# Two transformer blocks with a 32-expert layer: the experts' rows gathered already turned, in full precision, and six weight pieces loaded ahead instead of four

## The chip, the cores and the metric

The kernel runs on one core of a Trainium2 chip. The metric is the device time of one execution in microseconds (us); three runs are shown and the median counts. All times inside the execution are microseconds from the start of the profiled span.

## What is computed

The whole program is a first block of two mixers (gated spatial mixing with differential attention, then latent attention) over 512 tokens and 256 context rows, followed by a second block with grouped attention, retention and a mixture of experts. The change touches only the last stage, the experts:

```
grp_p = softmax(h @ w_grp + b_grp);  p_g, g_idx = top_k(grp_p, 1)
sel   = the 8 expert logits of that group
p_e, j_idx = top_k(softmax(sel), 2)                 # two experts a token
weights = p_g * (p_e / sum(p_e));  eid = g_idx * 8 + j_idx
...
y_blk = (silu(x_blk @ w_gate[e]) * (x_blk @ w_up[e])) @ w_down[e]
out[token] += y * weight
```

`h` is 512 tokens by 1024, all in f32; an expert has 512 hidden features, so its three matrices are 6 MiB in f32. There are 32 experts, and a token goes to two of them: 1024 assignments.

## The kernel before, in words

**Blocks.** Assignments are placed in blocks of 64 rows (`SLOT`). Blocks 0 to 31 belong to experts 0 to 31; what an expert gets beyond 64 rows goes to further blocks at the end. Blocks 0 to 29 are worked in 15 *pairs* (`PAIRS`), the rest as *singles*: block 30, 31 and, with the routing of these inputs, one more, 32 (33 first products in all).

**Weights.** An expert's matrices arrive as six pieces of 1 MiB (128 x 2048 f32), four for gate and up, two for down. The SP queue issues them. A ring of twelve buffers (`ring`, whose buffers have the tile names early, raw and ring) holds one pair. Four pieces are fetched before the experts start, the other eight once the earlier stages have freed their buffers. Then come `MORE` = 4 pieces of block 28, kept in four other buffers (`more`) until block 28 is worked, much later. After this, each ring buffer is filled again as soon as TensorE has used it (`s_used`, the loop at L688): SP waits for one piece, issues one transfer, and goes to the next. In the singles only the first six ring buffers are used (L701).

**Rows.** A block's rows are picked out of the normed rows `h2` (token tile m, 128 tokens on the partitions) by a one-hot matrix `hot` that VectorE makes (`one_hot`, L2047 and L2051). `in_product` contracts over the features, so it needs the rows turned, as `xe_t` (feature on the partition, row along it). Before the change this takes four steps for each pair (128 rows), or each single:

- once, ahead of the experts: ScalarE rounds `h2` to fp32r (`h2_high`, L1229), VectorE subtracts (`h2_low`, L1980), so that `h2h` + `h2l` are a high and a low part for fp32r products
- `gather(g, h)`, L2743: for each half h of the features, 4 token tiles x 2 parts = 8 products with `hot` stationary and 512 features moving, into one bank
- `gathered(g, h)`, L1248: ScalarE copies the bank to `xe_rows`
- `turn_rows(g, h)`, L2750: four transposes with the identity; `turned(g, h)`, L2078: VectorE copies to `xe_t`

**A pair on TensorE** (`pair(q, ...)`): `in_product` of block 2q (L2785, 16 f32 products, each two matmul records in the trace), `gather(q+1, 0)`, `turn_hidden` (L2794, two transposes of `hid`), `gather(q+1, 1)`, `out_product` (L2805, 8 products); then `in_product` of block 2q+1, `turn_rows(q+1, 0)`, `turn_hidden`, `turn_rows(q+1, 1)`, `out_product`. Between them ScalarE makes silu (L1252), VectorE multiplies (`hidden`, L2084), copies the turned `hid_t` (`hidden_turned`, L2088) and scales the output (`out_rows`, L2093). The result is stored to `pair_dram` by ScalarE's queue, for singles by GpSimd's. In `out_product` TensorE waits for `s_ht`, that is for the copy of L2088.

**The end.** After the last pair a table `late` is turned, the singles follow, the store of single 31 is awaited, GpSimd gathers all tokens' rows back from `pair_dram` (L872), and the last single's rows are added by a product (L2865). Then come the final norm and the stores.

Of the kernel before, what the change touches and what calls it, by code (L numbers as in the profile page):

```python
# [10 lines left out]
ALU = mybir.AluOpType  # L11
# [38 lines left out]
MORE = 4  # L50
# [253 lines left out]
def build(nc, src, out):  # L304
# [8 lines left out]
    with ExitStack() as stack:  # L313
# [67 lines left out]
        for g in range(2):  # L381
# [37 lines left out]
        h2h = at("h2h", xt_base, 0, [P, LT, D], F32R)  # L419
        h2l = at("h2l", xt_base, 16 * KB, [P, LT, D], F32R)  # L420
        h2_t = at("h2_t", xt_base, 32 * KB, [P, KT, SEQ])
        xe_rows = at("xe_rows", g_base, 16 * KB, [P, D])
        xe_t = at("xe_t", g_base, 44 * KB, [P, KT, P])
        hot = at("hot", xt_base, 40 * KB, [P, LT, P], F32R)
# [39 lines left out]
            ((gate_base, 0), (xt_base, 32), (g_base, 0), (g_base, 8)))]  # L464
# [100 lines left out]
        s_mods, s_row2, s_h2h, s_h2l = sem("s_mods"), sem("s_row2"), sem("s_h2h"), sem("s_h2l")  # L565
# [10 lines left out]
        s_first_hot, s_hot, s_gat, s_rows, s_turned, s_xt = (sem(n) for n in (  # L576
            "s_first_hot", "s_hot", "s_gat", "s_rows", "s_turned", "s_xt"))
# [72 lines left out]
        def _(sp):  # L650
# [230 lines left out]
        def _(act):  # L881
# [345 lines left out]
            def h2_high(m):  # L1227
                act.wait_ge(s_row2, m + 1)
                own.free(nc.scalar.activation(h2h[:, m, :], h2[:, m, :], ACT.Copy), s_h2h)  # L1229
# [15 lines left out]

            def gathered(g, h):
                act.wait_ge(s_gat, 2 * g + h + 1)
                nc.scalar.activation(xe_rows[:, 512 * h:512 * h + 512], ps[:, h, :], ACT.Copy).then_inc(s_rows, 1)  # L1248
# [15 lines left out]
            gathered(0, 0)  # L1264
            gathered(0, 1)
            act.wait_ge(s_blocks, 1)
            over = act.value_load(blocks_i[0:1, 40:41], min_val=0, max_val=BLOCKS - EXPERTS)
            with act.Fori(0, PAIRS) as q:
                silu(2 * q, 0)
                gathered(q + 1, 0)  # L1270
                gathered(q + 1, 1)
                store(2 * q, 0)
                silu(2 * q + 1, 1)
                store(2 * q + 1, 1)

            def single(o, nxt):
                silu(o + SINGLE, 0)
                if nxt:
                    gathered(o + PAIRS + 1, 0)
                    gathered(o + PAIRS + 1, 1)  # L1280
# [16 lines left out]
        def _(dve):  # L1297
# [679 lines left out]
            def h2_low(m):  # L1977

                dve.wait_ge(s_h2h, m + 1)
                own.free(nc.vector.tensor_tensor(h2l[:, m, :], h2[:, m, :], h2h[:, m, :].bitcast(F32), ALU.subtract), s_h2l)  # L1980

            for m in range(LT - 1):
                h2_low(m)

# [34 lines left out]
            h2_low(LT - 1)  # L2019
# [25 lines left out]
            def one_hot(g):  # L2045
# [4 lines left out]
                for m in range(LT):  # L2050
                    ins = nc.vector.scalar_tensor_tensor(hot[:, m, :], col, rel[:, bass.ds(8 * g + 4 + m, 1)],  # L2051
                                                         hot[:, m, :].bitcast(F32), ALU.is_equal, ALU.add)
# [23 lines left out]
            def turned(g, h):  # L2076
                dve.wait_ge(s_turned, 2 * g + h + 1)
                nc.vector.tensor_copy(xe_t[:, 4 * h:4 * h + 4, :], ps[:, 2 + h, :].rearrange("p (k n) -> p k n", k=4))\  # L2078
                    .then_inc(s_xt, 1)
# [50 lines left out]
            def single(o, nxt):  # L2130
# [46 lines left out]
        def _(pe):  # L2177
# [633 lines left out]
            pe.wait_ge(s_h2h, LT)  # L2811
            pe.wait_ge(s_h2l, LT)
            gather(0, 0)
            gather(0, 1)
            turn_rows(0, 0)
            turn_rows(0, 1)
# [3 lines left out]
            def pair(q, landed):  # L2820
# [18 lines left out]
            def single(o, nxt):  # L2839
                landed = single_piece(o)  # L2840
                in_product(o + PAIRS, 0, landed)
                if nxt:
                    gather(o + PAIRS + 1, 0)
                turn_hidden(o + SINGLE, 0)
                if nxt:
                    gather(o + PAIRS + 1, 1)
                out_product(o + SINGLE, 0, landed)
                if nxt:
# [133 lines left out]
```

## Time and profile before

| | |
|---|---|
| median of 3 runs | 1719.63 us (1715.76 to 1721.85) |
| span of the profiled execution | 1721.2 us, which lies within the runs |
| TensorE busy | 1585.1 us, 92% |
| VectorE / ScalarE / GpSimd busy | 927.7 / 517.6 / 157.0 us |
| expert stage, first in_product to the end | 1201.7 to 1721.2 us |
| transfers | 353.09 MB, 422 to 423 GB/s from 1240 to 1640 us |

The results give no time for the profiled execution apart from its span. Engines are TensorE (PE), its weight load (PEld), VectorE (DVE), ScalarE (ACT), GpSimd (POOL) and SyncE (SP). Matmul records overlap in the trace, so spacing between starts tells more than the duration of a record. A full-precision f32 product is two records of the same line.

### The profile page before, as it was taken

The numbers are of one execution on the slowest core, as the hardware profiler recorded it, in microseconds if no ns is written. First come the engines' busy times: TensorE is split into PE (matmuls) and PEld (weight loads), VectorE is DVE, ScalarE is ACT, GpSimd is POOL, SyncE is SP. The second block draws the span as 40 slices with busy tenths as digits, with TensorE's granted clock in tenths as the row PEclk, the third lists the DMA queues.
The fourth block names the chain that finished last, engine by engine and source line by source line (L and its number), as shares of the span: only waits on it lengthen the run. The fifth ranks groups of instructions, "written<-read, shape, count | busy, mean of one in ns | idle before, by whom it ended". The sixth has DMA issues, their size and how long they took to land.

```text
span 1721.2 us, 22873 instructions
## 1 busy us (share of the span) xinstructions
PE 1585.1 (92%) x8534; PEld 1112.6 (65%) x8534; DVE 927.7 (54%) x1602; ACT 517.6 (30%) x823; POOL 157.0 (9%) x203
## 2 busy tenths in 40 slices
PE   6699999979899999999999989899999898898995
PEld 6588887768688877878778868776434233333331
DVE  3877445466557854657679789777222212112124
ACT  3322221266615234454352368323000000000011
POOL 2000010013401100000132040110000000000003
PEclk9899999959999999999999999999999999999999
DMA  9132244300321421041445201257999999999995
GB/s 382 55 147 98 98 154 180 126 30 13 135 98 51 164 92 50 1 159 55 164 168 196 98 1 50 99 230 318 388 423 423 423 422 422 422 423 422 423 383 216
DMA packets 57620, 353.09 MB, mean 205 GB/s; under 512 B 7376, under 2 KB 7632, under 8 KB 20544
## 3 DMA queue, kind: packets, MB, share of 16 engines
q1 hardware_dynamic: 43200, 307.41, 44.6%
q0 software_dynamic: 9248, 35.63, 5.6%
q10 hardware_dynamic: 5088, 8.92, 1.4%
q8 instruction: 55, 0.90, 0.2%
q14 instruction: 29, 0.24, 0.0%
HBM read 332.53 MB, written 23.59 MB: 207 GB/s over the span
## 4 chain that ended last, share of the span: by engine, by line
PE 59%; DMA 16%; DVE 12%; ACT 5%; issue 3%; SPq 3%; POOL 1%; ACTq 0%; DVEq 0%; POOLq 0%
DMA early<-in_experts 11%; PE ps L2241 10%; PE ps L2243 10%; PE ps L2242 10%; PE ps L2785 7%; PE ps L2295 4%; PE ps L2805 3%; PE ps L2448 3%; PE ps L2743 2%; SPq L688 2%; PE ps L2472 2%; PE ps L2207 2%; PE ps L2465 1%; DMA early<-in_ada 1%; ACT p L966 1%
## 5 line engine op out<-in xcount | busy, mean ns | idle before, releaser
L2241 PE MATMUL ps<-whi,xth 128*128 128x512 f32 (+1 forms) x768 | 301.0, 392 | 3.1 <-DVE xtl L1712 1.8
L2243 PE MATMUL ps<-whi,xtl 128*128 128x512 f32 (+1 forms) x768 | 297.7, 388 | 0.0
L2242 PE MATMUL ps<-wlo,xth 128*128 128x512 f32 (+1 forms) x768 | 297.6, 387 | 0.0
L2785 PE MATMUL ps<-early,xe_t 128*64 128x512 f32 x904 | 207.6, 598 | 31.7 <-DMA early<-in_experts 25.9
L2785 PEld LDWEIGHTS ps<-early,xe_t 128*64 128x64 f32 x904 | 60.8, 136 | 172.6 <-issue 104.4
L2241 PEld LDWEIGHTS ps<-whi,xth 128*128 128x128 f32 x768 | 145.7, 190 | 33.6 <-DVE xtl L1712 3.5
L2243 PEld LDWEIGHTS ps<-whi,xtl 128*128 128x128 f32 x768 | 145.5, 190 | 29.5
L2242 PEld LDWEIGHTS ps<-wlo,xth 128*128 128x128 f32 x768 | 145.9, 190 | 28.3
L2084 DVE TENSOR_TENSOR hid<-hid,ps 128x256 f32<-128x256 f32 x33 | 13.9, 421 | 252.2 <-ACT hid L1252 252.2
L1308 DVE TENSOR_TENSOR wlo<-raw,whi 128x2048 fp32r<-128x2048 f32 (+3 forms) x52 | 103.2, 1984 | 71.4 <-ACT whi L893 70.7
L1252 ACT ACTIVATE hid<-ps 128x256 f32<-128x256 f32 x33 | 12.7, 385 | 392.5 <-PE ps L2785 392.5
L893 ACT ACTIVATE whi<-raw 128x2048 fp32r<-128x2048 f32 (+2 forms) x46 | 85.5, 1859 | 121.9 <-DMA raw<-in_even 34.1
L1355 DVE SCALAR_TENSOR_TENSOR raw<-raw,cvec 128x512 f32<-128x512 f32 x140 | 105.2, 752 | 5.0 <-DMA raw<-in_ada 0.2
L1601 DVE TENSOR_REDUCE stat<-ps 128x1 f32<-128x768 f32 x64 | 61.2, 957 | 55.8 <-PE ps L2465 51.4
L2093 DVE TENSOR_TENSOR tmp<-ps,gt 128x512 f32<-128x512 f32 x33 | 22.8, 692 | 105.7 <-PE ps L2805 105.7
L2805 PE MATMUL ps<-raw,hid_t 128*64 128x512 f32 x288 | 65.8, 598 | 0.6 <-DVE hid_t L2088 0.6
L723 POOL TENSOR_SCALAR stat<-stat 128x1 f32<-128x1 f32 (+3 forms) x39 | 18.5, 474 | 492.7 <-ACT xtl_f L1001 132.5
L2743 PE MATMUL ps<-h2h,hot 128*128 128x512 f32 x144 | 60.2, 418 | 0.0
L2743 PE MATMUL ps<-h2l,hot 128*128 128x512 f32 x144 | 56.5, 393 | 0.0
L1355 DVE SCALAR_TENSOR_TENSOR acc<-raw,cvec,acc 128x512 f32<-128x512 f32 x70 | 52.6, 752 | 2.9 <-DMA raw<-in_ada 0.4
L863 POOL DMA_DIRECT2D pair_dram<-tmp x4 | 2.2, 562 | 507.8 <-DVE tmp L2093 507.8
L1057 ACT ACTIVATE po<-ps,stat 128x768 f32<-128x768 f32 x32 | 28.9, 902 | 64.1 <-DVE stat L1601 64.1
(464 smaller groups left out, 2786.9 us busy)
## 6 DMA issues: line engine op xcount, KB each, us to landing
early<-in_experts SPq DMA_DIRECT2D x128, 1024.0 KB, 26.4
raw<-in_experts SPq DMA_DIRECT2D x51, 1024.0 KB, 25.2
raw<-in_ada SPq DMA_DIRECT2D x40, 1024.0 KB, 6.5
ring<-in_experts SPq DMA_DIRECT2D x15, 1024.0 KB, 27.7
raw<-in_even SPq DMA_DIRECT2D x14, 1024.0 KB, 5.1
raw<-in_second SPq DMA_DIRECT2D x10, 1024.0 KB, 5.2
early<-in_ada SPq DMA_DIRECT2D x8, 1024.0 KB, 18.2
pair_dram<-tmp ACTq DMA_DIRECT2D x60, 128.0 KB, 6.9
```

The source lines that it names most:

```text
L893: own(nc.scalar.activation(whi[:, k % SPLIT, 0:w], raw[:, number[splits[k]["name"]] % RAW, 0:w], ACT.Copy), s_hi)
L1308: own(nc.vector.tensor_tensor(wlo[:, k % SPLIT, at_], raw[:, g % RAW, at_], whi[:, k % SPLIT, at_].bitcast(F32), ALU.subtract), s_lo if pa ...
L1355: ins = nc.vector.scalar_tensor_tensor(dst, w[kt // 4][:, kt % 4, :], cv, dst, ALU.mult, ALU.add)
L1601: own(nc.vector.tensor_reduce(st[:, 1:2], v[:, 0:TOK], AX, ALU.max, negate=True), nb)
L2241: nc.tensor.matmul(v, a[0], b[0], start=first, stop=False)
L2242: nc.tensor.matmul(v, a[0], b[1], start=False, stop=False)
L2243: return nc.tensor.matmul(v, a[1], b[0], start=False, stop=last)
L2295: mm = nc.tensor.transpose(v[:, to:to + P], rows_, ident[:])
L2448: mm = nc.tensor.matmul(v[:, TOK:TOK + n], pts[w % 2][:, P * a:P * a + P], v_of(w, a), start=a == 0, stop=a == NT - 1)
L2743: mm = nc.tensor.matmul(ps[:, h, :], hot[:, m, :], part[:, m, 512 * h:512 * h + 512], start=m == 0 and part is h2h, stop=m == LT - 1 and p ...
L2785: mm = nc.tensor.matmul(ps[SLOT * t:SLOT * t + SLOT, 4 + s, :], xe_t[:, 2 * i + k, SLOT * s:SLOT * s + SLOT], w[:, D * k + 512 * t:D * k + ...
L2805: mm = nc.tensor.matmul(ps[SLOT * t:SLOT * t + SLOT, 7, :], hid_t[:, s, P * c + SLOT * k:P * c + SLOT * k + SLOT], w[:, D * k + 512 * t:D ...
```

## The change

`h2h`, `h2l` and `xe_rows` are gone, with the ScalarE and VectorE steps that made them. `gather` now has `h2` stationary (128 tokens x 128 features) and `hot` moving (128 or, in the singles, 64 columns), both in f32, and writes the turned rows straight into the bank from which `turned` copies: 2 halves x 4 feature groups x 4 token tiles = 32 products for each group of rows. In a pair the first half is gathered after the first block's `in_product`, the second after the second block's. `in_product` waits for each half of `xe_t` apart. In the singles `turned` copies 64 columns of each feature group. `MORE` is 6, the first four of these buffers lie where `h2h` and `h2l` were, and are waited for differently.

```diff
-MORE = 4
+MORE = 6
...
         more = [at(f"more{i}", base, offset * KB, [P, PIECE]) for i, (base, offset) in enumerate(
-            ((gate_base, 0), (xt_base, 32), (g_base, 0), (g_base, 8)))]
+            ((xt_base, 0), (xt_base, 8), (xt_base, 16), (xt_base, 24), (gate_base, 0), (xt_base, 32)))]
...
+            def kept(i):
+                sp.dma_start(more[i][:], src["experts"][SINGLE - 2, i]).then_inc(s_more, 16)
+
+            for i in range(3):
+                kept(i)
+            sp.wait_ge(s_sqn, SQUARED["h2", NT - 1])
+            kept(3)
             sp.wait_ge(s_row2, LT)
-            sp.dma_start(more[0][:], src["experts"][SINGLE - 2, 0]).then_inc(s_more, 16)
+            kept(4)
             filled(sp, "router")
-            sp.dma_start(more[1][:], src["experts"][SINGLE - 2, 1]).then_inc(s_more, 16)
-            for i in (2, 3):
-                sp.wait_ge(s_h2l, 2 * i - 2)
-                sp.dma_start(more[i][:], src["experts"][SINGLE - 2, i]).then_inc(s_more, 16)
+            kept(5)
...
-            turned_h2(2)
-            turned_h2(3)
-            h2_high(0)
-            h2_high(1)
-            turned_h2(4)
-            h2_high(2)
-            turned_h2(5)
-            h2_high(3)
+            for m in range(CT, NT):
+                turned_h2(m)
...
-                    turned(o + PAIRS + 1, 0)
-                    turned(o + PAIRS + 1, 1)
+                    turned(o + PAIRS + 1, 0, SLOT)
+                    turned(o + PAIRS + 1, 1, SLOT)
...
-            def gather(g, h):
-                pe.wait_ge(s_hot, g + 1)
-                for m in range(LT):
-                    for part in (h2h, h2l):
-                        mm = nc.tensor.matmul(ps[:, h, :], hot[:, m, :], part[:, m, 512 * h:512 * h + 512],
-                                              start=m == 0 and part is h2h, stop=m == LT - 1 and part is h2l)
-                mm.then_inc(s_gat, 1)
-
-            def turn_rows(g, h):
-                pe.wait_ge(s_rows, 2 * g + h + 1)
+            def gather(g, h, n=P):
+                if h == 0:
+                    pe.wait_ge(s_hot, g + 1)
                 for k in range(4):
-                    mm = nc.tensor.transpose(ps[:, 2 + h, P * k:P * k + P],
-                                             xe_rows[:, 512 * h + P * k:512 * h + P * k + P], ident[:])
+                    for m in range(LT):
+                        mm = nc.tensor.matmul(ps[:, 2 + h, P * k:P * k + n],
+                                              h2[:, m, 512 * h + P * k:512 * h + P * k + P], hot[:, m, 0:n],
+                                              start=m == 0, stop=m == LT - 1)
                 mm.then_inc(s_turned, 1)
...
-                pe.wait_ge(s_xt, 2 * g + 2)
                 for i in range(4):
+                    if i % 2 == 0:
+                        pe.wait_ge(s_xt, 2 * g + (i // 2 + 1))
...
             def pair(q, landed):
                 in_product(q, 0, landed)
                 gather(q + 1, 0)
                 turn_hidden(2 * q, 0)
-                gather(q + 1, 1)
                 out_product(2 * q, 0, landed)
                 in_product(q, 1, landed)
-                turn_rows(q + 1, 0)
+                gather(q + 1, 1)
                 turn_hidden(2 * q + 1, 1)
-                turn_rows(q + 1, 1)
                 out_product(2 * q + 1, 1, landed)
```

TensorE, last pair, from the end of the second block's `in_product` to its `out_product`. Before:

```order
L2785 MATMUL ps<-early,xe_t 64x512 [waits s_ew9]
L2785 MATMUL ps<-early,xe_t 64x512 x3
L2750 MATMUL ps<-ident,xe_rows 128x128 [waits s_rows]
L2750 MATMUL ps<-ident,xe_rows 128x128 x3
L2794 MATMUL ps<-ident,hid 128x128 [waits s_hid]
L2794 MATMUL ps<-ident,hid 128x128
L2750 MATMUL ps<-ident,xe_rows 128x128 [waits s_rows]
L2750 MATMUL ps<-ident,xe_rows 128x128 x3
L2805 MATMUL ps<-early,hid_t 64x512 [waits s_ew10,s_yev,s_ht]
```

The same place with the change (L2752 is in_product, L2715 gather, L2761 turn_hidden, L2772 out_product):

```order
L2752 MATMUL ps<-early,xe_t 64x512 [waits s_ew9]
L2752 MATMUL ps<-early,xe_t 64x512 x3
L2715 MATMUL ps<-hot,h_119 128x128 x16
L2761 MATMUL ps<-ident,hid 128x128 [waits s_hid]
L2761 MATMUL ps<-ident,hid 128x128
L2772 MATMUL ps<-early,hid_t 64x512 [waits s_ew10,s_yev,s_ht]
```

Eight transposes on both sides of `turn_hidden` became sixteen products ahead of it, and nothing stands between `turn_hidden` and the product that waits for `s_ht`. The first block of a pair now has the same order.

SP, from the last ring pieces to the loop. Before:

```order
L677 DMA ring_143<-in_experts 128x2048
L679 DMA more_144<-in_experts 128x2048 [waits s_row2]
L681 DMA more_145<-in_experts 128x2048 [waits s_mm2]
L684 DMA more_146<-in_experts 128x2048 [waits s_h2l]
L684 DMA more_147<-in_experts 128x2048 [waits s_h2l]
L688 ISA [waits s_used]
```

With the change:

```order
L673 DMA ring_140<-in_experts 128x2048
L676 DMA more_141<-in_experts 128x2048
L676 DMA more_142<-in_experts 128x2048
L676 DMA more_143<-in_experts 128x2048
L676 DMA more_144<-in_experts 128x2048 [waits s_sqn]
L676 DMA more_145<-in_experts 128x2048 [waits s_row2]
L676 DMA more_146<-in_experts 128x2048 [waits s_mm2]
L689 ISA [waits s_used]
```

Two more transfers stand ahead of the loop that fills the ring again, and three of them wait for nothing.

TensorE in the loop of singles, after the last products of `out_product`. Before:

```order
L2805 MATMUL ps<-raw,hid_t 64x512 x3
L2748 ISA
L2750 MATMUL ps<-ident,xe_rows 128x128 [waits s_rows]
L2750 MATMUL ps<-ident,xe_rows 128x128 x3
L2748 REGISTER_ALU
L2750 MATMUL ps<-ident,xe_rows 128x128 [waits s_rows]
L2750 MATMUL ps<-ident,xe_rows 128x128 x3
L2852 ISA
```

With the change, from the end of `turn_hidden`:

```order
L2761 MATMUL ps<-ident,hid 128x128
L2715 MATMUL ps<-hot,h_119 128x64 x16
L2772 MATMUL ps<-raw,hid_t 64x512 [waits s_ew4,s_yev,s_ht]
L2772 MATMUL ps<-raw,hid_t 64x512 x3
L2772 MATMUL ps<-raw,hid_t 64x512 [waits s_ew5]
L2772 MATMUL ps<-raw,hid_t 64x512 x3
L2810 ISA
```

The transposes after a single's `out_product` are gone; the second half's sixteen products, of 64 columns, stand ahead of it.

## Rows read from the trace of the kernel before

**Rows 1.** The page, share of busy transfer engines in 40 slices of 43 us.

```profile
DMA  9132244300321421041445201257999999999995
```

**Rows 2.** Windows: length; busy time (count) of PE, PEld, DVE, ACT, POOL; clock; DMA; GB/s.

```profile
1340.00:1600.00 260.00, 230.59 (x1034) 87.86 (x1034) 50.61 (x130) 16.72 (x34) 0.00 (x0) 1.00 1.01 423
```

**Rows 3.** Timeline of TensorE: first piece of pairs 5 and 6, idle time and its releaser.

```profile
1337.67 1.94 PE L2785 MATMUL ps<-early,xe_t 128*64 128x512 f32 x8 [0.35 <-DMA early<-in_experts]
...
1368.69 1.94 PE L2785 MATMUL ps<-early,xe_t 128*64 128x512 f32 x8 [0.46 <-DMA early<-in_experts]
```

**Rows 4.** Chain that ended last, start and length: first gather, pairs 0, 1, 14.

```profile
1195.84 3.69 PE ps L2743 x16
1201.73 7.09 PE ps L2785 x32
...
1229.01 6.87 PE ps L2785 x32
1235.88 2.04 PE ps L2743 x8
1238.14 1.85 PE ps L2743 x8
1239.99 3.58 PE ps L2805 x16
1243.58 6.89 PE ps L2785 x32
1252.44 3.65 PE ps L2805 x16
1256.09 6.87 PE ps L2785 x32
...
1616.42 6.87 PE ps L2785 x32
```

**Rows 5.** Timeline, last single: turn_hidden, its copy, out_product, nothing between them.

```profile
1688.72 0.44 PE L2794 MATMUL ps<-ident,hid 128*128 128x128 f32 x2 [1.04 <-DVE hid L2084]
1689.20 0.42 DVE L2088 COPY hid_t<-ps 128x256 f32<-128x256 f32 x1 [0.53 <-PE ps L2794]
1689.75 3.65 PE L2805 MATMUL ps<-raw,hid_t 128*64 128x512 f32 x16 [0.59 <-DVE hid_t L2088]
```

**Rows 6.** Timeline of TensorE and its weight loads: f32 products with 128 weights' columns.

```profile
1101.67 0.46 PE L2650 MATMUL ps<-state,qw_t 128*128 128x128 f32 x2 [0.72 <-issue]
...
1108.67 0.39 PE L2651 MATMUL ps<-vr,sw 128*128 128x128 f32 x2
...
1101.86 0.30 PEld L2651 LDWEIGHTS ps<-vr,sw 128*128 128x128 f32 x2
...
660.36 2.94 PE L2448 MATMUL ps<-v_o,pto 128*128 128x128 f32 x24
```

**Rows 7.** Chain: the router's products (36 columns moving). Timeline: products with 64 weights' columns.

```profile
1175.82 3.51 PE ps L2700 x32
...
1082.16 1.53 PE L2584 MATMUL ps<-ptg,kk 128*64 128x128 f32 x24 [0.26 <-ACT tmp L1185]
```

**Rows 8.** Windows of 2 us around the first refill of the ring.

```profile
1200.00:1202.00 2.00, 0.93 (x6) 0.62 (x8) 1.78 (x5) 0.15 (x1) 0.00 (x0) 1.00 0.68 287
1202.00:1204.00 2.00, 2.00 (x12) 0.67 (x10) 1.90 (x9) 0.00 (x0) 0.00 (x0) 1.00 0.06 16
1204.00:1206.00 2.00, 2.00 (x12) 0.66 (x10) 1.93 (x10) 0.00 (x0) 0.00 (x0) 1.00 0.53 115
```

**Rows 9.** Chain, the singles: in_product of 30 and 31, out_product of 31, the store.

```profile
1646.65 7.09 PE ps L2785 x32
...
1663.63 7.09 PE ps L2785 x32
...
1674.82 3.61 PE ps L2805 x16
...
1680.51 6.91 DMA pair_dram<-tmp
```

More of the change, by code:

```diff
@@ L418, in build @@
         shift_row = at("shift_row", g_base, 44 * KB, [P, D])
-        h2h = at("h2h", xt_base, 0, [P, LT, D], F32R)
-        h2l = at("h2l", xt_base, 16 * KB, [P, LT, D], F32R)
         h2_t = at("h2_t", xt_base, 32 * KB, [P, KT, SEQ])
-        xe_rows = at("xe_rows", g_base, 16 * KB, [P, D])
         xe_t = at("xe_t", g_base, 44 * KB, [P, KT, P])
-        hot = at("hot", xt_base, 40 * KB, [P, LT, P], F32R)
+        hot = at("hot", xt_base, 40 * KB, [P, LT, P])
         hid = at("hid", xt_base, 42 * KB, [P, 2, WIDTH // 2])
@@ L561, in build @@
         s_out = sem("s_out")
-        s_mods, s_row2, s_h2h, s_h2l = sem("s_mods"), sem("s_row2"), sem("s_h2h"), sem("s_h2l")
+        s_mods, s_row2 = sem("s_mods"), sem("s_row2")
         s_rcl, s_gd, s_ge, s_rw, s_chosen, s_blocks = (sem(n) for n in (
@@ L574, in build @@
         s_used = sem("s_used")
-        s_first_hot, s_hot, s_gat, s_rows, s_turned, s_xt = (sem(n) for n in (
-            "s_first_hot", "s_hot", "s_gat", "s_rows", "s_turned", "s_xt"))
+        s_first_hot, s_hot, s_turned, s_xt = (sem(n) for n in ("s_first_hot", "s_hot", "s_turned", "s_xt"))
         s_silu, s_hid, s_tr, s_ht = (sem(n) for n in ("s_silu", "s_hid", "s_tr", "s_ht"))
@@ L1244, in _ @@
             nc.scalar.preload_act_table(ACT.Silu)
-            def gathered(g, h):
-                act.wait_ge(s_gat, 2 * g + h + 1)
-                nc.scalar.activation(xe_rows[:, 512 * h:512 * h + 512], ps[:, h, :], ACT.Copy).then_inc(s_rows, 1)
             def silu(n, s):
@@ L1263, in _ @@
             act.wait_ge(s_fill, 16 * 8)
-            gathered(0, 0)
-            gathered(0, 1)
             act.wait_ge(s_blocks, 1)
@@ L1269, in _ @@
                 silu(2 * q, 0)
-                gathered(q + 1, 0)
-                gathered(q + 1, 1)
                 store(2 * q, 0)
@@ L1277, in single @@
                 silu(o + SINGLE, 0)
-                if nxt:
-                    gathered(o + PAIRS + 1, 0)
-                    gathered(o + PAIRS + 1, 1)
             v = filled(act, "late")
@@ L1976, in _ @@
             row(5)
[L1977 to L1983, printed above, removed]
             v = filled(dve, "router")
@@ L2018, in _ @@
             own(nc.vector.tensor_tensor(route[:, 16:20], top[2], top[1], ALU.subtract), s_gd)
-            h2_low(LT - 1)
             v = filled(dve, "counts")
@@ L2051, in one_hot @@
                     ins = nc.vector.scalar_tensor_tensor(hot[:, m, :], col, rel[:, bass.ds(8 * g + 4 + m, 1)],
-                                                         hot[:, m, :].bitcast(F32), ALU.is_equal, ALU.add)
+                                                         hot[:, m, :], ALU.is_equal, ALU.add)
                 ins.then_inc(s_hot, 1)
@@ L2074, in _, with turned @@
             own(nc.vector.tensor_tensor(pair_w[:, 4:8], pair_w[:, 0:4], route[:, 16:20], ALU.mult), s_rw)
-            def turned(g, h):
+            def turned(g, h, n=P):
                 dve.wait_ge(s_turned, 2 * g + h + 1)
-                nc.vector.tensor_copy(xe_t[:, 4 * h:4 * h + 4, :], ps[:, 2 + h, :].rearrange("p (k n) -> p k n", k=4))\
+                nc.vector.tensor_copy(xe_t[:, 4 * h:4 * h + 4, 0:n], ps[:, 2 + h, :].rearrange("p (k n) -> p k n", k=4)[:, :, 0:n])\
                     .then_inc(s_xt, 1)
@@ L2809, in out_product @@
                     mm.then_inc(s_used, 1)
-            pe.wait_ge(s_h2h, LT)
-            pe.wait_ge(s_h2l, LT)
             gather(0, 0)
             gather(0, 1)
-            turn_rows(0, 0)
-            turn_rows(0, 1)
             pe.wait_ge(s_blocks, 1)
@@ L2842, in single @@
                 if nxt:
-                    gather(o + PAIRS + 1, 0)
+                    gather(o + PAIRS + 1, 0, SLOT)
                 turn_hidden(o + SINGLE, 0)
                 if nxt:
-                    gather(o + PAIRS + 1, 1)
+                    gather(o + PAIRS + 1, 1, SLOT)
                 out_product(o + SINGLE, 0, landed)
-                if nxt:
-                    turn_rows(o + PAIRS + 1, 0)
-                    turn_rows(o + PAIRS + 1, 1)
             with pe.Fori(0, over + 1) as o:
```

3 lines of the change are left out of this document (removed).

## The prediction

> **What bounds the kernel now.** I read the page first: the last third has the transfer engines at nine tenths or more in every slice but the last [rows 1]. The windows give the rate there, 423 GB/s at full TensorE clock [rows 2]. Then the timeline of TensorE for who waits: from pair 5 on, each pair's first product waits for its weights, and pairs 5 and 6 start 31.02 us apart [rows 3]. That is the transfers' period: 12 pieces of 1.049 MB and 0.52 MB of stores, 13.1 MB at 423 GB/s. Then the chain for what TensorE alone needs: pair 1 to pair 2 is 1256.09 - 1229.01 = 27.08 us without a wait for weights [rows 4]. So two periods lie close, TensorE 27.1 and transfers 31.0. TensorE starts with a full ring, runs it down in five pairs, waits from there, and leads again only at pair 14, whose first pieces were kept since the start. From 1616.42 [rows 4] to the end the chain is TensorE's, then the store and the gather back. What matters is therefore whether the new TensorE period stays under 31, when TensorE can reach pair 14, and what it adds after that.
>
> **The new period, step by step.** Per pair the change removes 16 fp32r gather products, 2.04 + 1.85 = 3.89 us on TensorE [rows 4], and 8 transposes, the larger part of the time between the second block's two products; it adds 32 full-precision products, 64 records.
>
> Pace of a record: the retention products have the same form, 128x128 f32 weights and 128 columns moving, new weights for each. From 1101.67 to 1108.67 there are 62 records, with 2 more in the last row: 7.00/62 = 0.113 us [rows 6]. Another line of this form gives at most 2.94/24 = 0.1225 [rows 6]. The router's products, whose moving side is only 36 columns, still take 3.51/32 = 0.110 [rows 7]: here the weight load sets the pace, not the columns. I take 0.112 for 128 columns and 0.110 for 64: halving the columns in the singles buys next to nothing. Half a group is 32 records, 3.58 us, and about 0.1 us for entering full-width products after half-width ones (the first eight gather records take 2.04, the next eight 1.85 [rows 4], and part of that is the fp32r kind's): 3.68.
>
> The rows show a weight load starting at 1101.86, while the products that began at 1101.67 are in flight [rows 6]; loads and products overlap. The Trainium skill (TensorE: Matmul & The Clock Gate, Part 3: Packing small matmuls) says that a weight load overlaps products in flight only when its row group differs, which speaks against this change; by that rule each of the 64 full-array records would pay load and product in turn. It is the fourth rival below, and the trace so far disagrees with it.
>
> The second cost is a wait that the old order hid. `out_product` waits for the copy of `hid_t`. Before, half a gather (first block) or transposes (second block) stood after `turn_hidden`. Now nothing does. The last single already has that order: from `turn_hidden` to `out_product` 1689.75 - 1688.72 = 1.03 us [rows 5]. I take 1.0, twice per pair. The silu and its multiplication, on the other hand, are covered by the 3.7 us of gather ahead of `turn_hidden` in both blocks. VectorE has time for its copies and `one_hot` during the 3.65 us of `out_product`.
>
> New block: 6.88 in_product + 3.68 gather + 1.0 + 3.65 out_product [rows 4] = 15.2; **new pair 30.4 us**, 3.3 more than now, and 0.6 under the transfers' 31.02.
>
> **What the pieces ahead do.** Two more pieces cost 5.0 us of transfer (2.1 MB at 423 GB/s) before the first refill. Now the queue runs dry there: 1200 to 1206 moves 287, 16 and 115 GB/s in windows of 2 us [rows 8], together 0.84 MB where 2.54 MB would fit, 4.0 us idle. So the two pieces fill the hole and push the refills by about 1 us. They save nothing further on the critical side: they serve block 28, where TensorE already has its weights in time. Transfers then reach pair 13 at 1337.67 + 8 x 31.02 + 1 = 1586.8; TensorE reaches it at 1202.9 + 13 x 30.4 = 1598. The weights are ahead by 16 us at pair 5, 11 at pair 13. **TensorE becomes the bound of all 15 pairs.**
>
> **The sum**, against the span of 1721.2:
> - First product. The 16 fp32r records from 1195.84, the copy, the transposes and the wait end at 1201.73 [rows 4]. Now 63 records of 0.112 follow the first, 7.1 us, so 1202.9: +1.2. The removed rounding and subtraction cost nothing: the router's products kept TensorE busy beside them, and the last subtraction lay beside the counting products. The one-hot is not ready earlier.
> - Pairs 0 to 13: 14 x 30.4 = 425.6 in place of 1616.42 - 1201.73 = 414.7 [rows 4]: +10.9.
> - Pair 14: 30.4 for 27.1: +3.3. The turned `late` table is unchanged.
> - Single 30: now 1663.63 - 1646.65 = 16.98 [rows 9]. New: 7.09 + 3.63 + 0.2 (turn_hidden) + 3.52 + 3.61 = 18.1, then only VectorE's scaling and a copy of 256 columns before the next in_product, about 1.4: 19.5, +2.5. Here the second half-gather does hide the `hid_t` copy.
> - Single 31 to the end of its out_product: now 1674.82 + 3.61 - 1663.63 = 14.8 [rows 9], new 18.1: +3.3. The store after it takes 6.91 [rows 9], with loads of the last block in the queue; these are a little further on now. I take 0, bounds 0 and -1.5. The rest is as it was.
>
> Sum +21.2: a profile of 1742.4. The median of the runs lies 1.6 below the span, so **1741**.
>
> Bounds: columns alone would give 0.107 (in_product's 512 columns, two at a time, take 6.87/16 = 0.43 a record, a quarter of it for 128 [rows 4]). With that and no entry cost the period is 29.9, and the terms are +0.8, +3.9, +2.8, +2.2, +3.0: 1732. With 0.1225 a half is 4.0 us, the period 31.1, and they become +1.9, +20.7, +4.0, +3.3, +4.0: 1754.
>
> **Rivals.** An effect under 0.3%, 5 us, can't be told from none here.
> 1. *The transfers stay the bound.* If the period is under 29.6, pair 14 waits for the refills and starts near 1617.4 whatever TensorE does. For it: the periods differ by 2%. Against: the sum has to be wrong by 0.8 per pair, against three rows for the pace. Time: +1 for the refills, +2.5 for pair 14, +2.0, +2.8 for the singles: 1728.
> 2. *Not slower: the new products run at the half-width pace.* Products with 64 weights' columns take 1.53/24 = 0.064 a record [rows 7]. At r us a record, with transfers the bound, the sum is 1 + 192r - 12.2 (pair 14 and two singles, 64 records each), which falls under 5 us for r below 0.084; at 0.064 it is +1.1: 1721. Against: those run two at a time on half of the array, and the new ones fill it.
> 3. *Slower than forecast: waits that I left out.* Two more bubbles of about 0.7 per pair, for instance VectorE's copies of `xe_t` standing in the way of `hid_t`, or the sequencer at the two waits inside `in_product`: 31.8 per pair, +30.5 for pairs 0 to 13, +4.7 for 14, and +1.2, +3.2, +4.0 for the start and the singles: 1763.
> 4. *No overlap of load and product.* Load pace 0.110 and product 0.112 in turn [rows 6, 7] make 0.222 a record, 7.0 us more per group: 37.4 per pair, 14 x 37.4 - 414.7 = +108.9, and +8.2, +10.3, +9.5, +10.3 for the other terms: 1867. The Trainium skill's rule above is this case.
>
> **Chances.** Forecast 0.79; rival 1 0.07; rival 2 0.04; rival 3 0.08; rival 4 0.02. The range 1728 to 1754 holds the forecast with its bounds, and rival 1; most of rivals 2 to 4 and some of the forecast's edges are left out. Faster 0.02 and same 0.05 come from rival 2 and the lowest edge of rival 1; slower 0.93.
>
> **What would show it.** Right: no wait of in_product for expert weights in pairs 1 to 14; pairs 30.4 apart; 32 gather records in 3.6 to 3.7 us, for 64 columns as well; about 1.0 from turn_hidden to out_product; no hole in the transfers at 1202, but a rate under 423 GB/s later, since TensorE frees buffers too slowly; the out_product of single 31 ending 21 us later. Wrong: waits for weights at pair 10 or later (rival 1), a gather record far from 0.112 (2, 4), or other idle time on TensorE inside a pair (3).

## The result and the profile after

The changed kernel takes **1734.19 us** (median of 4 runs, 1733.02 to 1739.82) against 1718.55 for the kernel before, run beside it (4 runs). The ratio on record is **1.0105**, with a 95% interval of 1.0086 to 1.0124; the two medians alone give 1.0091, which lies inside it. So it is slower, by 15.6 us between the medians. The forecast was 1741, its range 1728 to 1754.

From the page of the changed kernel: the span and the share of busy transfer engines in 40 slices of 43 us, the last of which answers to [rows 1].

```profile
span 1731.3 us, 24235 instructions
...
DMA  9132245300322321043334202349999999999865
```

The transfers are still near full from slice 28 on, but they fall in the last three slices, where before only the last one fell. They are done early, and TensorE no longer waits for them. The waits of TensorE in the expert stage, 1190 to 1690 us, say who waits now. The columns are: who waits, for whom, us in total, times, longest.

```profile
PE ps L2772 <- DVE hid_t L2059: 15.5, 30, 0.5
PE ps L2752 <- ACT sin_t L1263: 2.6, 1, 2.6
PE ps L2752 <- DVE xe_t L2049: 1.3, 1, 1.3
```

For comparison, the same view of the kernel before:

```profile
PE ps L2785 <- DMA early<-in_experts: 25.9, 36, 1.2
PE ps L2794 <- DVE hid L2084: 7.8, 16, 1.0
...
PE ps L2805 <- DVE hid_t L2088: 0.6, 1, 0.6
```

25.9 us of waiting for weights and 7.8 us of waiting for `hid` have gone. In their place stand 30 waits of 0.52 us for the copy of the turned hidden rows, one in each block, and more work. The chain that ended last, in order of time, shows that work (start, length, what; it answers to [rows 4] and, from 1650.01 on, to [rows 9]).

```profile
1188.56 7.38 PE ps L2715 x64
1195.94 7.02 PE ps L2752 x32
...
1226.14 6.87 PE ps L2752 x32
1233.01 3.77 PE ps L2715 x32
1236.77 0.23 PE ps L2761 x2
1237.03 0.44 DVE hid_t L2059
1237.51 3.65 PE ps L2772 x16
1241.16 6.87 PE ps L2752 x32
...
1616.79 6.87 PE ps L2752 x32
...
1650.01 8.78 PE ps L2752 x32
1658.79 3.72 PE ps L2715 x32
1662.51 0.22 PE ps L2761 x2
1662.73 3.52 PE ps L2715 x32
...
1671.14 7.09 PE ps L2752 x32
...
1685.68 3.61 PE ps L2772 x16
```

One block is 1241.16 - 1226.14 = 15.02 us, without a gap that the weights made, and it is the same from block 1 to block 28: 30.05 us a pair, just under the transfers' 31.02. `gather` (L2715) is 3.77 us of it, and from `turn_hidden` (L2761) to `out_product` (L2772) it is 1237.51 - 1236.77 = 0.74.

Windows of the same kernel (length; busy time and count of PE, PEld, DVE, ACT, POOL; clock; DMA share; GB/s) answer to [rows 8] and [rows 2]:

```profile
1200.00:1202.00 2.00, 2.00 (x12) 0.64 (x10) 1.69 (x7) 0.00 (x0) 0.00 (x0) 1.00 0.99 418
1202.00:1204.00 2.00, 2.00 (x16) 1.19 (x13) 0.42 (x1) 0.38 (x1) 0.00 (x0) 1.00 0.96 360
1204.00:1206.00 2.00, 2.00 (x20) 2.00 (x19) 0.00 (x0) 0.00 (x0) 0.00 (x0) 1.00 1.03 418
1340.00:1600.00 260.00, 250.69 (x1424) 124.72 (x1424) 54.00 (x141) 6.51 (x17) 0.00 (x0) 1.00 1.01 423
1640.00:1680.00 40.00, 35.60 (x207) 19.19 (x206) 8.43 (x26) 2.64 (x7) 1.18 (x2) 0.96 0.58 212
1652.00:1654.00 2.00, 2.00 (x6) 0.51 (x4) 0.00 (x0) 0.00 (x0) 0.00 (x0) 0.50 0.44 66
```

The hole at 1202 is filled. The transfers keep 422 to 424 GB/s up to 1600 us, and at 1640 to 1680, with 212 GB/s, they have little left to do.

**Where the time went**, stage by stage, of the two profiled executions:

| stretch | before | after | difference | forecast |
|---|---|---|---|---|
| start to the one-hot ready | 1194.60 | 1188.41 | -6.2 | 0 |
| to the first product | 7.13 | 7.53 | +0.4 | +1.2 |
| pairs 0 to 13 | 414.7 | 420.8 | +6.2 | +10.9 |
| pair 14 and the late table | 30.2 | 33.2 | +3.0 | +3.3 |
| single 30 | 16.98 | 21.13 | +4.15 | +2.5 |
| single 31, to the end of its out_product | 14.80 | 18.15 | +3.35 | +3.3 |
| to the end | 42.8 | 42.0 | -0.8 | 0 |
| sum | 1721.2 | 1731.3 | +10.1 | +21.2 |

The first line is not the change's. The difference builds up in code that both kernels share: at 343 us the changed kernel's execution is already 3.7 us ahead, at 1000 us 6.1. The profiled execution of the kernel before was one of the longer ones; other executions of code that is nearly the same up to there (the three versions with pieces kept for pair 1, below) began their first product at 1193 to 1195 us, not 1201.7. Without that line the change costs 16.3 us in the profiles.

Two more lines hold something that the change did not do. In the kernel before, TensorE's granted clock was at half from 1188 to 1194 us, so that the products ahead of the gather (L2221) started 0.85 us apart in place of 0.43, and the gather behind them began late:

```profile
1190.00:1192.00 2.00, 2.00 (x3) 0.67 (x2) 1.77 (x7) 0.00 (x0) 0.00 (x0) 0.50 0.97 383
```

With the same gather and the clock back in time (the second and third of these versions) the first product came 6.2 us after the one-hot, not 7.13, which makes the change's share of that line +1.3. And 1.7 us of single 30's +4.15 are half clock in the changed kernel (last section). With both put right, 16.3 + 0.9 - 1.7 = 15.5 us, in keeping with the 15.6 of the medians. The three runs of the kernel before spread over 6 us all the same, so the agreement is no finer than that.

### The profile page after: what moved, and what is told of

Read it like the earlier page. It is cut to its first block, busy times and chain, and to the rows that moved or that the text cites. A ratio compares the mean times of both kernels' runs of the same rounds, so it can differ in the third digit from the quotient of the medians.

```text
span 1731.3 us, 24235 instructions
## 1 busy us (share of the span) xinstructions
PE 1617.0 (93%) x9254; PEld 1174.9 (68%) x9254; DVE 921.3 (53%) x1598; ACT 491.5 (28%) x783; POOL 155.8 (9%) x203
## 4 chain that ended last, share of the span: by engine, by line
PE 75%; DVE 12%; ACT 4%; DMA 4%; issue 3%; POOL 1%; SPq 0%; DVEq 0%; ACTq 0%; POOLq 0%
PE ps L2752 13%; PE ps L2212 11%; PE ps L2214 10%; PE ps L2213 10%; PE ps L2715 8%; PE ps L2772 7%; PE ps L2266 4%; PE ps L2419 3%; PE ps L2443 2%; PE ps L2178 2%; DMA early<-in_ada 1%; PE ps L2436 1%; ACT p L967 1%; DVE stat L1479 1%; DVE p L1491 1%
## 5 line engine op out<-in xcount | busy, mean ns | idle before, releaser
L2752 PE MATMUL ps<-early,xe_t 128*64 128x512 f32 x904 | 201.3, 597 | 5.2 <-DVE xe_t L2049 2.6
L2752 PEld LDWEIGHTS ps<-early,xe_t 128*64 128x64 f32 x904 | 65.2, 138 | 135.1 <-issue 135.0
L2715 PEld LDWEIGHTS ps<-hot,h 128*128 128x128 f32 x1152 | 131.3, 192 | 28.2 <-issue 28.2
L2715 PE MATMUL ps<-hot,h 128*128 128x128 f32 (+1 forms) x1152 | 137.5, 278 | 1.5 <-DVE hot L2022 1.5
L894 ACT ACTIVATE whi<-raw 128x2048 fp32r<-128x2048 f32 (+2 forms) x46 | 85.5, 1858 | 118.1 <-DMA raw<-in_even 33.2
L2772 PE MATMUL ps<-raw,hid_t 128*64 128x512 f32 x272 | 62.1, 598 | 7.8 <-DVE hid_t L2059 7.8
L2059 DVE COPY hid_t<-ps 128x256 f32<-128x256 f32 x33 | 14.0, 425 | 88.7 <-PE ps L2761 88.7
## 6 DMA issues: line engine op xcount, KB each, us to landing
early<-in_ada SPq DMA_DIRECT2D x8, 1024.0 KB, 18.6
```

The source lines that it names most:

```text
L894: own(nc.scalar.activation(whi[:, k % SPLIT, 0:w], raw[:, number[splits[k]["name"]] % RAW, 0:w], ACT.Copy), s_hi)
L2715: mm = nc.tensor.matmul(ps[:, 2 + h, P * k:P * k + n], h2[:, m, 512 * h + P * k:512 * h + P * k + P], hot[:, m, 0:n], start=m == 0, stop=m ...
L2752: mm = nc.tensor.matmul(ps[SLOT * t:SLOT * t + SLOT, 4 + s, :], xe_t[:, 2 * i + k, SLOT * s:SLOT * s + SLOT], w[:, D * k + 512 * t:D * k + ...
L2772: mm = nc.tensor.matmul(ps[SLOT * t:SLOT * t + SLOT, 7, :], hid_t[:, s, P * c + SLOT * k:P * c + SLOT * k + SLOT], w[:, D * k + 512 * t:D ...
```

## The experiments

Nine kernels were run. Five try the parts of the change by themselves or beside an alternative, four ask what pieces loaded ahead can be worth. All ratios are to the kernel before, run beside them on the same chip (17 runs each time, medians 1716.7 to 1717.4). Stretches here go by the start of the first record in TensorE's timeline, which for the kernel before gives 414.5 us for pairs 0 to 13 and 30.4 for pair 14 with the late table, and for the changed kernel 420.8 and 33.4, some 0.2 off the chain's in the table.

### Four pieces ahead

```diff
-MORE = 6
+MORE = 4
...
-            kept(4)
...
-            kept(5)
```

> The changed kernel with four pieces kept ahead instead of six; the new gather stays. If TensorE bounds all 15 pairs (my theory): no wait of in_product for expert weights, first in_product to the start of pair 14 again 420.9 us (within 0.5), a hole of 3 to 5 us in the transfers around the first refill, and the time within 2 us of the changed kernel, 1.009 to 1.011 of before. If the six pieces pay: about 5 us slower than the changed kernel, with waits for weights in the later pairs. If they are what costs: 3 to 5 us faster.

Measured: 1733.99 us, ratio 1.0091 (1.0075 to 1.0106). Pairs 0 to 13 take 420.75 us, the same as with six pieces, and no product waits for weights. The hole in the transfers is back, as these windows of 2 us show:

```profile
1194.00:1196.00 2.00, 2.00 (x18) 1.78 (x19) 0.19 (x1) 0.00 (x0) 0.00 (x0) 1.00 0.58 234
1196.00:1198.00 2.00, 2.00 (x12) 0.67 (x10) 1.97 (x8) 0.00 (x0) 0.00 (x0) 1.00 0.04 16
1198.00:1200.00 2.00, 2.00 (x12) 0.62 (x10) 1.90 (x10) 0.00 (x0) 0.00 (x0) 1.00 0.59 102
```

It costs nothing, since TensorE at 30.05 us a pair never catches up with the transfers. The theory's signs and its ratio came as expected. The two more pieces are worth nothing in this kernel, and the whole loss belongs to the new gather.

### The copy of hid_t behind half of a gather

```diff
-                gather(q + 1, 0)
+                gather(q + 1, 0, ks=(0, 1))
                 turn_hidden(2 * q, 0)
+                gather(q + 1, 0, ks=(2, 3))
```

and the same in the pair's second block.

> The changed kernel with turn_hidden put into the middle of each pair's half-gather, so that 16 records follow it and cover the copy of hid_t. My theory: each block gets 0.45 to 0.5 us shorter (15.03 to 14.55), a pair 29.1 us, which is under the transfers' 31.02; waits for weights come back from about pair 10, and pair 14 starts where the transfers allow, about 5 us earlier than in the changed kernel; with 1 us of pair 14 the gain is 6 us: 1.006 to 1.008 of before. Rival, the exposed copy costs nothing because the engine would wait anyway: same time as the changed kernel.

Measured: 1728.18 us, ratio 1.0057 (1.0041 to 1.0073). The chain shows blocks of 1251.79 - 1237.35 = 14.44 us, with nothing between `turn_hidden` (L2762) and `out_product` (L2773) but the rest of the gather:

```profile
1237.35 6.87 PE ps L2753 x32
1244.21 1.98 PE ps L2715 x16
1246.20 0.22 PE ps L2762 x2
1246.41 1.79 PE ps L2715 x16
1248.20 3.58 PE ps L2773 x16
1251.79 6.87 PE ps L2753 x32
```

That is 0.58 us less a block, 16 us over the 28 blocks of pairs 0 to 13. But those pairs take 417.3 us in place of 420.8, only 3.5 less. At 28.9 us a pair TensorE is too fast for the transfers, and the waits for weights return, first at 1431 us, in pair 8 (a pair of 29.1 us and waits from about pair 10 were expected):

```profile
PE ps L2753 <- DMA early<-in_experts: 7.7, 12, 0.7
```

This is what rival 1 describes. That the time is also its 1728 is in part luck: its sum was 8.3 us over the kernel before, and this kernel is 10.8 over the one beside it. The run also shows how near the changed kernel is to the transfers' bound: about 3.5 us over 14 pairs, or 4.7 by the quarter of the gather below.

### 128 columns in the singles too

```diff
-                    gather(o + PAIRS + 1, 0, SLOT)
+                    gather(o + PAIRS + 1, 0)
...
-                    gather(o + PAIRS + 1, 1, SLOT)
+                    gather(o + PAIRS + 1, 1)
```

> The changed kernel with 128 instead of 64 columns moving in the two gathers of the singles. If the weight load sets the pace of a record: each half-gather of the singles stays within 0.1 us (3.72 and 3.52 now, 3.77 and 3.57 then), the singles 0.2 us longer in all. If the moving columns set it: 64 records x 0.05 us, 3.4 us longer for each of the two.

Measured: 1735.02 us in one run. The halves of the gather in single 30 of this kernel:

```profile
1659.56 3.77 PE ps L2715 x32
...
1663.55 3.57 PE ps L2715 x32
```

against 3.72 and 3.52 us with 64 columns. Twice the columns cost 0.10 us on 7.24, so the columns don't set the pace of these products. That agrees with the router's 0.110 us a record at 36 columns [rows 7]. That it is the weight load, and not another cost that each record has, is not separated by a run; for it speaks that the loads are busy for 2.00 of 2.00 us in the window from 1204 above.

### The old parts, turned directly

The kernel before, with its `h2h` and `h2l` stationary and the fp32r one-hot moving, so that the rows come out turned as in the change, and four pieces ahead:

```diff
...
-                        mm = nc.tensor.matmul(ps[:, h, :], hot[:, m, :], part[:, m, 512 * h:512 * h + 512],
+                            mm = nc.tensor.matmul(ps[:, 2 + h, P * k:P * k + n],
+                                                  part[:, m, 512 * h + P * k:512 * h + P * k + P], hot[:, m, 0:n],
...
```

> The kernel before with its high and low fp32r parts kept, but gathered like the changed kernel: parts stationary in 128 x 128, one-hot moving, turned rows straight into the bank, no ScalarE copy, no transposes; four pieces ahead. If each record pays a weight load of 0.112 us whatever its precision: 64 records for a group again, half-gathers of 3.6 to 3.8 us, pairs 0 to 13 at 420 to 421 us, a time like the changed kernel's. If full precision is what costs: half-gathers clearly under 3 us and pairs 0 to 13 near 415.

Measured: 1731.34 us in one run, 14.5 over the median of the kernel before. The chain, with the same half of a gather in L2738:

```profile
1411.27 3.72 PE ps L2738 x32
1414.99 0.25 PE ps L2784 x2
1415.27 0.43 DVE hid_t L2081
1415.75 3.65 PE ps L2795 x16
1419.40 6.87 PE ps L2775 x32
1426.27 3.72 PE ps L2738 x32
```

3.72 us where the changed kernel has 3.77. A high and a low part in fp32r, or one full-precision product of two records, come to the same. What costs is the turned shape: for each half, 32 records of 128 columns with new weights for each, in place of 8 of 512 columns and 4 transposes. The columns are the same 4096 in both, and 8 records of 512 took 1.85 us [rows 4], 32 of 128 take 3.72. Pairs 0 to 13 take 420.1 us, as the expectation has it.

### A quarter of the gather

The changed kernel with the first of the four token tiles alone; the rows of the other 384 tokens are left out.

```diff
-                    for m in range(LT):
+                    for m in range(1):
...
-                                              start=m == 0, stop=m == LT - 1)
+                                              start=True, stop=True)
```

> The changed kernel with only the first of the four token tiles gathered, so rows of the other 384 tokens are left out: 16 records in place of 64 for a group. TensorE's pair falls to 24.7 us, well under the transfers. Then the transfers set the floor for pair 14's start: pairs 0 to 13 at 416 to 418 us, as in split_gather, though TensorE is 4 us quicker per pair; pair 14 24.7, singles about 14.1 us each, 19 to 20 us less than the changed kernel in all. If TensorE's work set the time alone, pairs 0 to 13 would take 346 us.

Measured: 1708.32 us in one run, 25.9 under the changed kernel and 8.5 under the kernel before beside it. The expected 19 to 20 us left out the first gather and the clock. By stretches, against the changed kernel: 3.7 us less from the one-hot to the first product, 4.7 in pairs 0 to 13, 4.8 in pair 14, 6.8 in single 30 (5.1 against executions without the clock's dip that is told of below) and 5.1 in single 31. The waits of TensorE, 1190 to 1690 us:

```profile
PE ps L2752 <- DMA early<-in_experts: 46.7, 66, 1.0
PE ps L2772 <- DVE hid_t L2059: 16.0, 31, 0.5
...
PE ps L2761 <- DVE hid L2055: 1.0, 1, 1.0
```

With 48 records less in each group, 2.5 us less in each block, pairs 0 to 13 come down to 416.1 us and no further: from pair 3 on they are 31.0 us apart, with a full transfer queue. So with six pieces ahead no gather, however cheap, gains more than 4.7 us there. The kernel before, with four, is lower still, at 414.5: the prediction has the two extra pieces push the refills by about 1 us, and where the transfers are the bound that would count. No run has a quarter of the gather and four pieces, so it is not shown. In the last pair and the singles, where no transfer holds TensorE up, nearly all of what is saved counts.

### Pieces kept for pair 1 instead of pair 14

In the kernel before, the four kept pieces serve block 28 at the end, where TensorE is not late. Three versions use them for block 2. The first refills the ring from its fifth buffer on:

```diff
-                sp.dma_start(more[i][:], src["experts"][SINGLE - 2, i]).then_inc(s_more, 16)
-            with sp.Fori(1, PAIRS - 1) as q:
+                sp.dma_start(more[i][:], src["experts"][2, i]).then_inc(s_more, 16)
+            for i in range(MORE, 2 * PARTS):
+                sp.wait_ge(s_used, i + 1)
+                sp.dma_start(ring[i], src["experts"][2 + i // PARTS, i % PARTS]).then_inc(s_ew[i], 16)
+            for i in range(MORE):
+                sp.dma_start(ring[i], src["experts"][4, i]).then_inc(s_ew[i], 16)
...
```

> The kernel before, old gather, with the four kept pieces used for block 2 (pair 1) instead of block 28. If transfers bound pairs 5 to 14 when TensorE's period is 27.1: the transfers now also pace pair 14, whose last piece is the 164th of the refills and lands 16 x 2.586 us after the 148th (1594.1), at 1635.5, so pair 14 ends at about 1637.4 in place of 1643.5: 6 us faster than before, 0.996 to 0.997. Rival, TensorE sets the end of the pairs in the kernel before: no change or slower, since pair 14 gets waits that it did not have.

Measured: 1721.14 us, ratio 1.0020 (1.0008 to 1.0032), the wrong side of 1. The refill is one queue in order, and its first entry now waits for the fifth piece to be used. From 1196 to 1208 us nothing moves (the first and the last of six such windows):

```profile
1196.00:1198.00 2.00, 2.00 (x12) 0.69 (x10) 1.90 (x11) 0.00 (x0) 0.00 (x0) 1.00 0.00 0
...
1206.00:1208.00 2.00, 2.00 (x12) 0.72 (x10) 0.00 (x0) 0.22 (x1) 0.00 (x0) 1.00 0.00 0
```

The expectation had left that queue out. It isn't what the time went to, though: pairs 0 to 13 take 414.1 us, as in the kernel before. Pair 14 with the late table takes 33.7 in place of 30.4 and single 30 17.4 in place of 17.0, together the 0.2%: pair 14 got waits for weights that it didn't have, as the rival says. What the hole took, by comparison with the next version, is the gain that pairs 0 to 13 didn't get.

The second version fills the ring's first four buffers as soon as each is used, with block 4's pieces (the diff is to the first version):

```diff
-            for i in range(MORE, 2 * PARTS):
+            for i in range(2 * PARTS):
                 sp.wait_ge(s_used, i + 1)
-                sp.dma_start(ring[i], src["experts"][2 + i // PARTS, i % PARTS]).then_inc(s_ew[i], 16)
-            for i in range(MORE):
-                sp.dma_start(ring[i], src["experts"][4, i]).then_inc(s_ew[i], 16)
+                sp.dma_start(ring[i], src["experts"][(4 if i < MORE else 2) + i // PARTS, i % PARTS]).then_inc(s_ew[i], 16)
...
```

> The kernel before with the four kept pieces used for pair 1, and the first refills of the ring (pair 2's first four pieces) issued ahead of pair 1's other eight, so that the hole in the transfers is 4 us again and not 14. If that hole was why the first try gained nothing: first product to the end of pair 14 falls from 441.8 to 434 to 436 us, 0.9955 to 0.9975 of before. If the pairs' end is set by something else than the transfers: 441 to 442 us and no change.

Measured: 1716.83 us, ratio 0.9998 (0.9986 to 1.0010), not the expected gain. Pairs 0 to 13 do take 410.0 us, 4.5 less than the 414.5 of the kernel before, but pair 14 with the late table takes 33.7 where it took 30.4: 3.3 given back. From the first product to the end of pair 14 it is 440.5 us, nearer to the 441 to 442 of no change than to the 434 to 436 of the theory. Single 30 takes 18.6 where it took 17.0, but that is the clock and not the pieces: its granted clock fell to half, and its `in_product` took 8.78 us in place of 7.09.

```profile
1638.86 8.78 PE L2788 MATMUL ps<-early,xe_t 128*64 128x512 f32 x32 [2.57 <-ACT sin_t L1286]
```

What is left, 1.2 us, is less than the runs can tell. And there is a second hole, while block 2 runs from the kept buffers and no buffer of the ring comes free:

```profile
1230.00:1232.00 2.00, 2.00 (x12) 1.60 (x11) 0.69 (x2) 0.56 (x1) 0.00 (x0) 1.00 0.78 325
1232.00:1234.00 2.00, 2.00 (x11) 1.18 (x11) 0.08 (x1) 0.53 (x2) 0.00 (x0) 1.00 0.03 12
1234.00:1236.00 2.00, 2.00 (x12) 0.60 (x10) 0.00 (x0) 0.11 (x1) 0.00 (x0) 1.00 0.00 0
```

The split gather with six pieces kept in the same way:

> The new gather, split around turn_hidden, with its six kept pieces used for pair 1 and the refills ordered as in kept_early. My theory: TensorE's 28.9 us bounds all 15 pairs once the transfers are out of the way: first product to the end of pair 14 at 433 to 436 us (446.2 in split_gather), singles 19.45 us as there, 0.997 to 1.000 of before. Rival, transfers still bound: above 440 us with many waits for weights, 1.003 or more.

Measured: 1725.01 us, ratio 1.0055 (1.0036 to 1.0073), as the split gather alone. Pairs 0 to 13 take 412.9 us in place of 417.3, pair 14 with the late table 34.4 in place of 32.2, single 30 21.1 in place of 19.4, which is again the clock's dip. The same exchange. The expected 0.997 to 1.000 fell and the rival held: from the first product to the end of pair 14 it is 444.1 us, with 10 waits for weights.

The third version loads the four kept buffers again once block 2 has used them, with the pieces of block 28 (the diff is to the second version):

```diff
+            for i in range(MORE):
+                sp.wait_ge(s_used, 2 * PARTS + i + 1)
+                sp.dma_start(more[i][:], src["experts"][SINGLE - 2, i]).then_inc(s_more, 16)
             for i in range(MORE, 2 * PARTS):
                 sp.wait_ge(s_used, 2 * PARTS + i + 1)
                 sp.dma_start(ring[i], src["experts"][4 + i // PARTS, i % PARTS]).then_inc(s_ew[i], 16)
...
```

> The kernel before, with its four kept pieces used for block 2 and then loaded again with the first four pieces of block 28. Theory (in the version with the pieces kept for block 2 alone, no ring buffer comes free while block 2 runs, which is the second hole of 5 us in its transfers, and the 3.3 us lost at pair 14 and 1.7 us at single 30 are that hole, paid where the transfers are the last bound): the second hole of 1232 to 1237 us is gone, pair 14 with the late turn is back at 30.4 us and single 30 at 17.0 us. As the bytes between the first product and single 31 are then those of the kernel before, and the first hole stays at 3 to 4 us, the ratio to the kernel before is 0.998 to 1.000. Rival (the kept pieces for block 2 gain 4.5 us of waits in pairs 0 to 13 for good, and pair 14 was late for another reason): pairs 0 to 13 take 410 us and pair 14 30.4 us, ratio 0.996 to 0.997. Second rival: the four loads set in at block 2 push the ring's pieces back so far that a wait of over 2 us shows up between blocks 4 and 8, and the ratio is 1.000 or over.

Measured: 1716.54 us, ratio 1.0003 (0.9991 to 1.0015). The second hole is gone:

```profile
1232.00:1234.00 2.00, 2.00 (x12) 0.72 (x10) 0.00 (x0) 0.24 (x1) 0.00 (x0) 1.00 1.03 434
```

Pair 14 with the late table is back at 30.42 us, single 30 at 16.98, and pairs 0 to 13 are back at 413.3. So pair 14 came back as the theory has it, and the rival, 410 and 30.4 together, fell. Single 30 is no evidence: its 1.7 us in the second version were the clock, not the hole that the expectation put them down to. The ratio is just above the expected 0.998 to 1.000, with those inside its interval; the second rival's long wait did not come (the longest wait for weights is 1.3 us). What the four pieces save early they nearly all cost late, or they are loaded again and cost it at once: from the first product to the end of pair 14 it is 440.6 us, against 440.5 and the 441.8 of before. Whether the second hole by itself cost anything isn't separated: this version took the hole away and put four more loads among the pairs in one step.

No version that does the whole gather beat the kernel before.

## Why the prediction was right, and where its terms were off

The direction, the mechanism (TensorE becomes the bound of all 15 pairs, at a period between its old one and the transfers') and the range held. The forecast's sum of +21.2 us was 5.6 more than the 15.6 measured. By its own steps:

- **The pace of a record: right, and low by 2%.** 32 records were to take 3.68 us with the 0.1 for entering; they take 3.77, that is 0.118 each. The first gather's 64 take 7.38, 0.115.
- **"About 1.0" from turn_hidden to out_product: the mis-sized term.** It measures 0.74: 0.23 of two transposes, 0.44 of the copy, the rest signals. In the last single, from which it was taken [rows 5], the copy began 0.48 us after the first transpose, and TensorE had stood still for 1.04 us before it; in the pairs, where the transposes follow the gather at once, it begins 0.26 after. With 28 blocks in pairs 0 to 13 that is 7.3 us too many, and 28 x 0.09 = 2.5 too few from the gather: together the 4.7 us by which pairs 0 to 13 were overestimated. That the wait would be there, 30 times, was right, and the split gather shows what it costs: with the wait covered a block is 0.58 us shorter, 0.51 of it between `turn_hidden` and `out_product` and 0.07 in `out_product`.
- **First product +1.2: right, once the clock is taken out.** The profiles give +0.4, but the row that the sum started from, the old gather at 1195.84, was late by the half clock told of above. Against the versions where it wasn't it is +1.3. The 64 records took 7.38 us where 7.1 were forecast. That the removed rounding and subtraction cost nothing was right too: from the same retention product (1101.67 and 1095.50 us) to the one-hot it is 92.9 us in both kernels.
- **Pair 14 +3.3 and single 31 +3.3: right** (+3.0, +3.35). Single 30 +2.5: the two kernels with the same code there and no dip of the clock, the split gather and the 128-column one, took 19.44 and 19.54, which is +2.5. The profiled execution's +4.15 has 1.7 us of half clock in its `in_product`.
- **The silu is covered by the gather: right.** No wait for `hid` is left; with a quarter of the gather, one came back.
- **"A rate under 423 GB/s later": wrong, and it contradicted the text's own numbers.** With TensorE's period of 30.05 under the transfers' 31.02 the transfers are the slower of the two for as long as there are pieces to fetch, so they run at full rate, and only their lead shrinks, by 1 us a pair. What fell was the rate from 1600 on (400, 389, 125 and 299 GB/s in windows of 20 us), where the last pair and the singles ask for few pieces.
- **Two more pieces save nothing: right**, and shown by themselves (medians of 1733.99 us with four and 1734.19 with six; ratios 1.0091 and 1.0105, intervals overlapping).
- **Rivals.** 2 (half-width pace) and 4 (load and product in turn) fell with 0.118 us a record. 3 (more waits) fell, as the only wait inside a block is the one forecast. 1 (transfers stay the bound) did not happen here, but it was near: 0.6 us less in a block brought it on at pair 8.

On rival 4: the window of 1204 to 1206 us above has weight loads and products both busy for 2.00 us of 2.00, all of them 128 x 128. The Trainium skill (TensorE: Matmul & The Clock Gate, Part 3: Packing small matmuls) has a load overlap the products in flight only where its row group differs. In this kernel full-array loads and products run side by side, at 0.118 us a record where in turn it would be 0.22, and the measurement decides. The same section of the Trainium skill also has a load pulled ahead of products in flight where it goes to the background weight buffer; the trace is in keeping with that, but no run here shows which buffer the loads went to.

## What to carry to other kernels

A product that saves a copy and a transpose by coming out turned pays for it in records: count the weights that have to be loaded, not the columns, as 64 columns were hardly cheaper than 128. What TensorE does between two steps that depend on each other (here half a gather in one block of a pair, four transposes in the other) may be what hides another engine's copy; when it goes, put other work in that place. And before adding buffers to a stage that two engines bound by turns, see at which step the lead is used up: pieces loaded ahead move the wait, and here they moved it to where it cost the same.

## What was not expected of the hardware

**The columns are nearly free below 128.** 64 records take 7.24 us at 64 columns and 7.34 at 128, in the same place of the same program.

**The clock can fall after a short idle time.** Before single 30 TensorE waits 2.58 us for the turned `late` table. In the changed kernel's profiled execution the granted clock is then 0.80, 0.50 and 0.85 of full speed in the windows of 2 us from 1650 on, that is, it fell to the lower of its two levels, 1.2 GHz, and came back, and `in_product` takes 8.78 us in place of 7.09:

```profile
1650.01 8.78 PE L2752 MATMUL ps<-early,xe_t 128*64 128x512 f32 x32 [2.58 <-ACT sin_t L1263]
```

The versions with four pieces ahead, with the old parts turned directly, and with the split gather and six kept pieces did the same (20.9 to 21.4 us for single 30), and so did the second version of the kernel before with kept pieces (18.6). The other six profiled executions kept their clock after a wait of the same length or longer (2.84 us with a quarter of the gather), among them the first and third version with kept pieces, which have the same products there as the second. So it isn't the gather that decides; what does isn't settled. It is worth 1.4 to 1.7 us in an execution, more than several of the differences asked about here, and a stretch that holds such a fall must not be read as the effect of an edit.
